# An encoder layer on one core: GpSimd splits and half a projection inside attention, and a reordered LN1 stage

## The chip, the cores and the metric

One core of a Trainium2 chip runs the whole kernel in one launch. The metric is device time in microseconds (us). A core has TensorE (PE: matmuls; PEld is its weight loads), VectorE (DVE), ScalarE (ACT), GpSimd (POOL) and SyncE (SP, which here only issues DMAs). Each works through its own instructions in order; semaphores tie them together. On chip, data lies in SBUF and matmul results in PSUM, which has eight banks of 128 x 512 f32.

## What is computed

The reference, cut to what matters (one layer, 1024 tokens of width 1024):

```
proj = x @ w_in                      # u | v | q
y_pool = pool_mixer(u)               # window means minus token, small matmul
y_conv = silu(LN(dwconv31(a * sigmoid(gate)) + b_dw))     # a, gate = split(v)
y_mem  = softmax(q k^T / sqrt(128)) v                     # 4 heads, 256 memory tokens
x = LN(alpha * x + concat(y_pool, y_conv, y_mem) @ w_out) # "LN1"
scores = sigmoid(x @ w_router); top-8 of 64 experts, gates normalised
x = LN(alpha * x + sum_experts gate * swiglu_e(x) + swiglu_shared(x))
```

## The kernel before

The 1024 tokens are 8 tiles of 128 (`NT = 8`). For accuracy every f32 operand of the large matmuls is kept as two parts, `hi` (rounded to the matmul's f32r format) and `lo` (the rest), and each product is three matmuls, hi·hi, hi·lo and lo·hi (`PRODS`). ScalarE makes the `hi` parts with a copy; the `lo` part is a subtraction, on VectorE nearly everywhere. So an operand passes ScalarE, then VectorE or GpSimd, before TensorE can read it.

All orders are written out by hand: each engine's block is a straight program, and what is said below is where its steps stand.

**Input projections.** `JOBS` lists 20 steps, the last six being q0, q1, pool0, pool1, q2, q3. For each weight block ScalarE's `split_hi` (L664) and VectorE's `split_lo` (L960) make `whl`. VectorE computes the depthwise convolution's 31 taps for two channel blocks between them (L1046, each 128 x 1024 from `glu` and `cv`), and the pooling sums. When the taps are done VectorE raises `s_cvd`.

**Attention.** For each tile t: ScalarE `q_hi` (L726) and `q_lo` (VectorE, L1120) split the query; TensorE `scores` (L1555, 12 matmuls of 128 x 256); VectorE `row_max` (L1126, L1129); ScalarE `exps` (L734); VectorE `probabilities` (L1143, two 128 x 512 products of two SBUF tensors); TensorE transposes them (L1579) into banks 4 and 5; ScalarE and VectorE make `pT` hi (L761) and lo (L1165). After tiles 3 and 7 the four heads' outputs are computed (L1591, 24 matmuls of 128 x 512 into banks 6 and 7 by turns), and ScalarE's `attention_out` (L743) takes them out. Between these steps lie the convolution's LayerNorm: `conv_mean` (PE L1528), `centre` (DVE L1093), `centred_squares` (ACT), `conv_variance` (PE L1536), `spread_rstd` (DVE L1103), `conv_rows` (PE L1544), `scale` (DVE L1109), and `conv_out` (ACT L712), which finishes `mixA`. In steps 4 to 7 the output weights `wo` are split in four quarters, `wo_hi` (ACT L717) and `wo_lo` (DVE L1115, 128 x 2048). GpSimd waits for `conv_out`, then makes constants and writes the empty lists with 11 DMAs (L540).

**LN1 stage.** For each tile: `mix_hi` (ACT) and `mix_lo` (POOL L552) split the mixed operand `mst`, in two halves (`mixA` and `qT`); `project` (PE L1604) is 24 matmuls of 128 x 512 for each of two column halves; VectorE adds the residual and takes statistics (L1252, L1255, L1259, L1261), GpSimd's `rstd` (L545) gives the inverse deviation, VectorE finishes x1 (L1264, L1267). TensorE transposes x1 (L1470, `x1_transposed`), ACT and DVE split it into `x1T` (L790, L1175, `x1_lo`), then TensorE runs the shared expert's gate and up (L1640, 24 matmuls of 128 x 512) and the router's `logits` (L1629, 24 of 128 x 64). VectorE's `route` (L1204 to L1225) picks experts, TensorE's `ranks` counts, VectorE's `rank` (L1182 to L1197) makes list addresses, and GpSimd's `scatter` writes them with 8 indirect DMAs for a tile (L559). PE's order in a step t is project(t+1, 0), ranks(t-1), project(t+1, 1), x1_transposed(t), shared_gate_up(t-1), logits(t).

**Experts.** When all lists are written, GpSimd reads them and gathers rows (L634, L605), and TensorE goes through the 64 experts' items (L1697, L1715).

## Time and profile before

| | |
|---|---|
| median of 3 runs | 1415.71 us (1411.47 to 1418.12) |
| the profiled execution, whole | 1413.44 us |
| its span, first to last instruction | 1411.8 us |
| TensorE busy | 1321.9 us, 94% of the span |
| VectorE, ScalarE, GpSimd busy | 68%, 57%, 33% |
| mean granted TensorE clock | 0.963 of 2.4 GHz |

The span is what the trace covers; 1.6 us of the execution lie around it. Times below are microseconds from the span's start. A row of the timeline gives start, duration, engine, line and operation, what is written and read, and, in brackets, how long the engine was idle just before and what released it. A row of merged instructions has their count behind an x. Rows of a window's table give busy time and count for each engine, then the mean granted clock, the DMA engines' share and GB/s.

### The profile page before, as it was taken

The numbers are of one execution on the slowest core, as the hardware profiler recorded it, in microseconds if no ns is written. First come the engines' busy times: TensorE is split into PE (matmuls) and PEld (weight loads), VectorE is DVE, ScalarE is ACT, GpSimd is POOL, SyncE is SP. The second block draws the span as 40 slices with busy tenths as digits, with TensorE's granted clock in tenths as the row PEclk, the third lists the DMA queues.
The fourth block names the chain that finished last, engine by engine and source line by source line (L and its number), as shares of the span: only waits on it lengthen the run. The fifth ranks groups of instructions, "written<-read, shape, count | busy, mean of one in ns | idle before, by whom it ended". The sixth has DMA issues, their size and how long they took to land.

```text
span 1411.8 us, 25745 instructions
## 1 busy us (share of the span) xinstructions
PE 1321.9 (94%) x6395; PEld 1092.1 (77%) x6396; DVE 960.6 (68%) x1121; ACT 797.7 (57%) x1056; POOL 471.7 (33%) x432
## 2 busy tenths in 40 slices
PE   8989776899997999999999999999999999999974
PEld 6877565688885888888888888888888888788851
DVE  5898886567673695865778457546759579677727
ACT  4122266212233686775777557547769678677724
POOL 0000002346654333433344333333334343433421
PEclk9999876899998999999999999999999999999988
DMA  6121202323357898988899889788889899999665
GB/s 242 45 75 60 119 1 97 105 76 90 87 168 219 313 355 292 359 254 284 276 328 358 254 252 287 236 260 264 287 291 345 259 331 335 341 328 301 196 179 233
DMA packets 77970, 324.13 MB, mean 230 GB/s; under 512 B 22560, under 2 KB 24768, under 8 KB 52720
## 3 DMA queue, kind: packets, MB, share of 16 engines
q1 hardware_dynamic: 43056, 251.05, 47.9%
q0 software_dynamic: 33728, 68.47, 20.7%
q10 hardware_dynamic: 1152, 4.19, 0.9%
q8 instruction: 17, 0.28, 0.1%
q14 instruction: 17, 0.14, 0.0%
HBM read 290.51 MB, written 67.72 MB: 254 GB/s over the span
## 4 chain that ended last, share of the span: by engine, by line
PE 64%; DMA 2%; issue 1%; DVE 1%; ACT 1%; ACTq 0%; SPq 0%; POOL 0%; POOLq 0%; DVEq 0%
PE ps L1697 38%; PE ps L1715 18%; PE ps L1470 6%; PE ps L1728 1%; DMA sum_d<-ysb,idx 1%; DMA late__121<-sum_d 1%; DVE acc L1427 0%; DMA xg<-x_d,idx 0%; DVE acc L1430 0%; DMA idx<-list_d 0%; DVE acc L1446 0%; ACT sq L930 0%; SPq L491 0%; ACT wgu L773 0%; POOL rs L654 0%
## 5 line engine op out<-in xcount | busy, mean ns | idle before, releaser
L1697 PE MATMUL ps<-wgu,xTe 128*128 x2304 | 551.9, 395 | 2.8 <-ACT wgu L773 1.2
L1697 PEld LDWEIGHTS ps<-wgu,xTe 128*128 128x128 f32 x2304 | 427.9, 189 | 90.9 <-issue 5.0
L615 POOL DMA_INDIRECT sum_d<-ysb,idx x95 | 176.6, 1859 | 512.1 <-ACT ysb L845 440.9
L1715 PE MATMUL ps<-wdn,hT 128*128 (+1 forms) x1236 | 299.7, 392 | 2.6 <-ACT hT L808 2.6
L1338 DVE TENSOR_TENSOR wgu<-raw,wgu (+1 forms) x128 | 287.6, 2288 | 8.5 <-issue 3.4
L1715 PEld LDWEIGHTS ps<-wdn,hT 128*128 128x128 f32 x1236 | 232.7, 189 | 51.3 <-ACT hT L808 3.0
L773 ACT CAST wgu<-raw (+1 forms) x128 | 246.8, 1929 | 7.1 <-SPq L430 4.9
L1343 DVE TENSOR_TENSOR xTe<-ps,xTe 128x512 fp32r<-128x512 f32 x194 | 124.4, 683 | 136.8 <-ACT xTe L840 136.8
L1338 DVE TENSOR_TENSOR wdn<-raw,wdn x64 | 146.7, 2292 | 59.1 <-ACT wdn L833 59.1
L845 ACT ACTIVATE ysb<-ps,idx 128x512 f32<-128x512 f32 x188 | 119.2, 686 | 118.6 <-PE ps L1715 118.6
L605 POOL DMA_INDIRECT xg<-x_d,idx x99 | 112.6, 1137 | 47.4 <-issue 32.8
L833 ACT CAST wdn<-raw x64 | 124.8, 1951 | 0.0
L891 ACT ACTIVATE hs<-ps 128x256 f32<-128x256 f32 x96 | 36.9, 384 | 146.2 <-PE ps L1697 146.2
L840 ACT CAST xTe<-ps 128x512 fp32r<-128x512 f32 x194 | 104.3, 598 | 11.4 <-PE ps L1470 11.0
L1495 PE MATMUL ps<-xT,whl 128*128 128x512 f32 x480 | 110.1, 390 | 0.0
L1470 PE MATMUL ps<-ident,xg 128*128 128x128 f32 x776 | 102.2, 275 | 5.4 <-DMA xg<-x_d,idx 3.4
L1470 PEld LDWEIGHTS ps<-ident,xg 128*128 128x128 f32 x776 | 91.6, 141 | 18.7 <-DMA xg<-x_d,idx 3.9
L1495 PEld LDWEIGHTS ps<-xT,whl 128*128 128x128 f32 x480 | 89.9, 188 | 19.2 <-issue 0.4
L1372 DVE TENSOR_TENSOR hx<-hs,ps 128x256 f32<-128x256 f32 x96 | 40.0, 417 | 93.1 <-ACT hs L891 93.0
L1604 PE MATMUL ps<-wo,mst 128*128 128x512 f32 x384 | 95.3, 409 | 4.0 <-POOL mst L552 4.0
L559 POOL DMA_INDIRECT list_d<-tg,addr x64 | 75.1, 1174 | 61.0 <-DVEq L1199 44.3
L1604 PEld LDWEIGHTS ps<-wo,mst 128*128 128x128 f32 x384 | 74.9, 198 | 20.2 <-issue 4.4
(230 smaller groups left out, 1149.8 us busy)
## 6 DMA issues: line engine op xcount, KB each, us to landing
raw<-in_w_gate SPq DMA_DIRECT2D x64, 1024.0 KB, 10.9
raw<-in_w_up SPq DMA_DIRECT2D x64, 1024.0 KB, 8.5
raw<-in_w_down SPq DMA_DIRECT2D x64, 1024.0 KB, 8.6
wraw<-in_w_in SPq DMA_DIRECT2D x10, 512.0 KB, 3.4
xin<-in_x SPq DMA_DIRECT2D x8, 512.0 KB, 7.4
wraw<-in_w_kv SPq DMA_DIRECT2D x8, 512.0 KB, 3.2
wor<-in_w_out SPq DMA_DIRECT2D x4, 1024.0 KB, 8.0
xres<-in_x SPq DMA_DIRECT2D x8, 512.0 KB, 5.2
```

Of the source, the lines that this page charges most:

```text
L605: g.indirect_dma_start(out=xg[:, c % 2], out_offset=None, in_=x1_d, in_offset=bass.IndirectOffsetOnAxis(ap=idx[:, c % RING, 0:1], axis=0), ...
L615: g.indirect_dma_start(out=sums, out_offset=bass.IndirectOffsetOnAxis(ap=idx[:, c % RING, c % 2:c % 2 + 1], axis=0), in_=ysb[:, c % 2], in ...
L773: nc.scalar.copy(wgu[:, v, 0, :, n * XD:(n + 1) * XD].rearrange("p a c n -> p (a c) n"), raw[:, bass.ds(slot_of(e, n), 1)].rearrange("p a ...
L833: nc.scalar.copy(wdn[:, v, 0].rearrange("p a c n -> p (a c) n"), raw[:, bass.ds(slot_of(e, 2), 1)].rearrange("p a (c n) -> p (a c) n", c=2 ...
L845: nc.scalar.activation(ysb[:, slot, b * 512:(b + 1) * 512], ps[:, bank + b, :], ACT.Copy, scale=scale).then_inc(s_y, 1)
L1338: V.tensor_tensor(dst, raw_, hi.bitcast(F), ALU.subtract).then_inc(done, 1)
L1343: last = V.tensor_tensor(xTe[:, s, 1, 4 * b:4 * b + 4], ps[:, b, :].rearrange("p (c n) -> p c n", c=4), xTe[:, s, 0, 4 * b:4 * b + 4].bitc ...
L1470: last = nc.tensor.transpose(ps[:, bank + c // 4, (c % 4) * 128:(c % 4 + 1) * 128], src[:, c * 128:(c + 1) * 128], ident[:])
L1495: last = mm(ps[:, b + h, :], wt[:, st, d], xT[:, mo, d, h * 512:(h + 1) * 512], start=(d == 0 and st == 0 and mo == 0), stop=(d == ND - 1 ...
L1604: last = mm(ps[:, 5 + h, :], mst[:, t % 2, st, c], wo[:, mo, c, h * 512:(h + 1) * 512], start=(c == 0 and st == 0 and mo == 0), stop=(c == ...
L1697: last = mm(ps[:, 2 + s, :], xTe[:, s, st, d], wgu[:, w, mo, d].rearrange("p a n -> p (a n)"), start=(d == 0 and st == 0 and mo == 0), sto ...
L1715: last = mm(ps[:, down_bank(i) + h, :], hT[:, s, st, c], wdn[:, w, mo, c, h * 512:(h + 1) * 512].rearrange("p a n -> p (a n)"), start=(c = ...
```

## The change

Two groups of edits.

*Attention.* The q and `wo` lo parts move from VectorE to GpSimd; `wo`'s quarters are loaded and split in the order 2, 3, 0, 1, starting in step 0. The fourth and last query weights' `split_hi(17)` stands before pool0's evacuation, no longer at q2. The mixed operands of tiles 0 and 1 get buffers of their own (`mst0`, `mst1`), and the half from `qT` (blocks 4 to 7) is split as soon as the first group's heads are out. TensorE runs blocks 4 to 7 of tile 0's projection in steps 4 and 5, into banks 6 and 7, and blocks 0 to 3 after the second group of heads. `scores(6)` and `scores(7)`, `conv_variance` and `conv_rows`, `variance`, `spread_rstd`, `scale` and `conv_out` stand at other steps. The second group's heads go to four banks (2, 3, 0, 1) and wait for no evacuation. GpSimd issues the list fills after its last `wo_lo`, and the constants after that. SP loads the first two residual tiles when the taps are done.

*LN1 stage.* TensorE's order in a step becomes project(t+1, 0), x1_transposed(t), ranks(t-1), project(t+1, 1), logits(t), shared_gate_up(t-1), with a written-out start. VectorE does `x1_lo(t-1)` right after the first half's statistics, `route` before `shared_hidden`, and the shared weights' lo (`shared_lo`) after the first `route`. ScalarE splits the shared weights after `x1_hi(0)`.

```
-                if w in W_JOBS and W_JOBS.index(w) < 17:
+                if w == "pool0":
+                    split_hi(17)
+                elif w in W_JOBS and W_JOBS.index(w) < 16:
                     split_hi(W_JOBS.index(w) + 1)
...
+            for t in range(4):
+                q_lo(t)
+            wo_lo(1, 2)
+            q_lo(4)
+            wo_lo(2, 3)
+            q_lo(5)
             g.wait_ge(s_norm_v, 1)
             g.tensor_tensor(rv[:, 1], rv[:, 0], half8[:], ALU.pow).then_inc(s_rstd, 1)
-
-            g.wait_ge(s_mix, 2)
+            q_lo(6)
+            q_lo(7)
+            wo_lo(3, 0)
+            mix_lo_half(1, 0, slice(4, 8))
+            mix_lo_half(2, 1, slice(4, 8))
+            wo_lo(4, 1)
+
+            for first in range(S, LIST, 8192):
...
+            g.wait_ge(s_norm_pe, 3)
...
-            mix_lo(0)
-            mix_lo(1)
-            g.wait_ge(s_fill, 16 * -(-(LIST - S) // 8192))
+            mix_lo_half(3, 0, slice(0, 4))
+            mix_lo_half(4, 1, slice(0, 4))
...
             for t in range(NT):
-                if t + 2 < NT:
-                    scores(t + 2)
-                if t == 1:
-                    conv_variance()
-                if t == 3:
-                    conv_rows()
-                    pe.wait_ge(s_yn, 1)
...
+                if t < 4:
+                    scores(t + 2)
+                if t == 4:
+                    scores(7)
+                probabilities_transposed(t)
+                if t == 1:
+                    conv_variance()
+                if t == 3:
+                    scores(6)
+                    pe.wait_ge(s_norm_v, 1)
+                    heads_out(0)
+                if t == 4:
+                    pe.wait_ge(s_wolo, 2)
+                    pe.wait_ge(s_olo, 1)
+                    pe.wait_ge(s_oe, HEADS)
+                    project_part(0, 0, range(4, 8), True, False)
+                if t == 5:
+                    project_part(0, 1, range(4, 8), True, False)
+                if t == 6:
+                    conv_rows()
+            heads_out(1)
+            pe.wait_ge(s_wolo, 4)
+            pe.wait_ge(s_olo, 3)
+            for h in range(2):
+                project_part(0, h, range(4), False, True).then_inc(s_pre_h if h == 0 else s_pre_pe, 1)
...
+            for t in range(2, NT - 1):
+                project(t + 1, 0)
                 x1_transposed(t)
...
+                ranks(t - 1)
+                project(t + 1, 1)
                 logits(t)
+                shared_gate_up(t - 1)
```

ScalarE at the end of the input projections, before: the split `whl<-wraw` of q3's weights is the row behind the two pool evacuations (`mixA`).

```order
L700 COPY qT<-ps 128x1024
L664 CAST whl<-wraw 128x1024
L700 COPY qT<-ps 128x1024
L703 ACTIVATE mixA<-ps,cpar 128x1024 x2
L664 CAST whl<-wraw 128x1024
L700 COPY qT<-ps 128x1024 x2
```

After:

```order
L744 COPY qT<-ps 128x1024
L706 CAST whl<-wraw 128x1024
L744 COPY qT<-ps 128x1024
L706 CAST whl<-wraw 128x1024
L747 ACTIVATE mixA<-ps,cpar 128x1024 x2
L744 COPY qT<-ps 128x1024 x2
```

The split now stands before both pool evacuations.

GpSimd from the end of its opening constants through attention, before:

```order
L523 TENSOR_TENSOR rv<-rv,half_143 128x8
L526 IOTA listE 128x64
L528 IOTA tokf 128x2
L530 IOTA itemp 128x2
L532 IOTA tg 128x64
L533 IOTA tg 128x64
L534 MEMSET ones_106 128x65
L535 MEMSET cumf 128x64
L536 MEMSET cumb 128x128
L540 DMA list_d<-fillw 128x192 x10
L540 DMA list_d<-fillw 128x96
L552 TENSOR_TENSOR mst<-mixA,mst 128x512
```

After, the same stretch up to the list fills; the iotas and memsets follow these, and then the `mixA` halves of tiles 0 and 1:

```order
L539 TENSOR_TENSOR qst<-qT,qst 128x512
L544 TENSOR_TENSOR wo<-wor,wo 128x2048
L539 TENSOR_TENSOR qst<-qT,qst 128x512
L561 TENSOR_TENSOR rv<-rv,half_145 128x8
L539 TENSOR_TENSOR qst<-qT,qst 128x512 x2
L544 TENSOR_TENSOR wo<-wor,wo 128x2048
L551 TENSOR_TENSOR mst_75<-qT,mst_75 128x512
L551 TENSOR_TENSOR mst_76<-qT,mst_76 128x512
L544 TENSOR_TENSOR wo<-wor,wo 128x2048
L571 DMA list_d<-fillw 128x192 x10
L571 DMA list_d<-fillw 128x96
```

GpSimd has twelve new splits, and the fills stand ahead of what TensorE's remaining half projection waits for.

VectorE in the LN1 stage after the change, from the start of tile 1 to the part of tile 2 that feeds the second logits (L1301 is the shared weights' lo, L1231 is `x1_lo`; of `route` only its last row, L1281, is shown, the ten ahead of it are left out):

```order
L1310 SCALAR_TENSOR_TENSOR xres<-xres,ps 128x512
L1313 BN_STATS stat<-xres 128x6
L1319 BN_AGGR mv<-stat 128x2
L1321 TENSOR_SCALAR mv<-mv 128x1
L1324 SCALAR_TENSOR_TENSOR xres<-xres,mv,g_86 128x1024
L1327 SCALAR_TENSOR_TENSOR xres<-xres,rs,b_87 128x1024
...
L1281 TENSOR_SCALAR msc<-msc,gs 128x64
L1301 TENSOR_TENSOR wsh<-wshr,wsh 128x8x256 x2
L1310 SCALAR_TENSOR_TENSOR xres<-xres,ps 128x512
L1313 BN_STATS stat<-xres 128x6
L1231 TENSOR_TENSOR x1T<-ps,x1T 128x512 x2
```

Before, the `wsh` rows stood ahead of tile 0's first row, and `x1T` behind each tile's L1261.

## Rows read from the trace of the kernel before

**Rows 1.** The page, part 1: busy us, share of the span, instructions.

```profile
PE 1321.9 (94%) x6395; PEld 1092.1 (77%) x6396; DVE 960.6 (68%) x1121; ACT 797.7 (57%) x1056; POOL 471.7 (33%) x432
```

**Rows 2.** Windows: busy us (instructions) by engine, PEclk, DMA share, GB/s.

```profile
165.00:174.00 9.00, 0.00 (x0) 0.00 (x0) 8.63 (x8) 2.59 (x4) 0.00 (x0) 0.70 0.96 381
183.00:211.00 28.00, 19.54 (x115) 16.81 (x113) 25.69 (x47) 17.49 (x46) 2.03 (x1) 0.79 0.00 1
211.00:251.00 40.00, 24.67 (x104) 19.48 (x104) 21.64 (x30) 27.83 (x53) 9.38 (x21) 0.71 0.28 98
251.00:276.00 25.00, 24.58 (x96) 20.09 (x97) 13.05 (x13) 4.86 (x4) 8.17 (x6) 0.87 0.31 106
276.00:297.00 21.00, 18.62 (x87) 15.52 (x86) 13.88 (x30) 3.60 (x6) 3.35 (x4) 0.84 0.20 76
460.00:1360.00 900.00, 895.98 (x4405) 750.16 (x4404) 614.55 (x575) 624.27 (x763) 342.69 (x286) 1.00 0.88 291
```

**Rows 3.** Timeline, end of the input projections, ScalarE's and VectorE's rows.

```profile
143.39 1.04 ACT L664 CAST whl<-wraw 128x1024 fp32r<-128x1024 f32 x1
144.46 1.22 DVE L960 TENSOR_TENSOR whl<-wraw,whl 128x1024 fp32r<-128x1024 f32 x1 [5.95 <-ACT whl L664]
158.88 14.49 DVE L1046 SCALAR_TENSOR_TENSOR cv<-glu,wdw,cv 128x1024 f32<-128x1024 f32 x11
```

**Rows 4.** Timeline, TensorE, attention and the first projection.

```profile
174.28 5.12 PE L1555 MATMUL ps<-kT,qst 128*128 128x256 f32 x24 [10.15 <-DVE qst L1120]
179.23 3.60 PE L1528 MATMUL ps<-cv,ones 128*128 128x512 f32 x8
...
186.69 1.26 PE L1579 MATMUL ps<-ident,pr 128*128 128x128 f32 x8 [2.44 <-DVE pr L1143]
...
206.40 1.97 PE L1579 MATMUL ps<-ident,pr 128*128 128x128 f32 x8 [2.94 <-DVEq L1111]
211.18 5.40 PE L1591 MATMUL ps<-pT,vv 128*128 128x512 f32 x12 [2.82 <-DVE pT L1165]
...
251.42 24.77 PE L1604 MATMUL ps<-wo,mst 128*128 128x512 f32 x96 [3.99 <-POOL mst L552]
```

**Rows 5.** Timeline, VectorE and GpSimd instructions that overlap, in the LN1 stage.

```profile
269.03 2.31 DVE L1267 SCALAR_TENSOR_TENSOR xres<-xres,rs,b 128x1024 f32<-128x1024 f32 x1 [0.47 <-POOL rs L545]
270.22 2.27 POOL L552 TENSOR_TENSOR mst<-qT,mst 128x512 fp32r<-128x512 f32 x1
...
308.37 2.89 DVE L1225 TENSOR_SCALAR msc<-msc,gs 128x64 f32<-128x64 f32 x1
308.67 1.29 POOL L552 TENSOR_TENSOR mst<-mixA,mst 128x512 fp32r<-128x512 f32 x1
```

**Rows 6.** Instructions writing `wo` and `mst`: ns min/median/max; then one timeline row.

```profile
L1115 DVE TENSOR_TENSOR wo<-wor,wo x4: 2278/2281/2291, 225.5 to 240.5; 128x2048 fp32r<-128x2048 f32 x4
L552 POOL TENSOR_TENSOR mst<-mixA,mst x8: 1263/1292/1721, 248.8 to 369.1; 128x512 fp32r<-128x512 f32 x8
...
214.10 6.14 POOL L540 DMA_DIRECT2D list_d<-fillw  x11 [0.32 <-POOL cumb L536]
```

**Rows 7.** Timeline, start of the LN1 stage, TensorE and VectorE.

```profile
259.57 4.49 DVE L1242 TENSOR_TENSOR wsh<-wshr,wsh 128x2048 fp32r<-128x2048 f32 x2 [7.74 <-ACT wsh L817]
279.45 3.76 PE L1629 MATMUL ps<-wrt,x1T 128*128 128x64 f32 x24 [2.38 <-DVE x1T L1175]
283.02 8.07 PE L1604 MATMUL ps<-wo,mst 128*128 128x512 f32 x24
...
305.50 5.71 PE L1604 MATMUL ps<-wo,mst 128*128 128x512 f32 x24
```

**Rows 8.** Timeline, the last addresses (VectorE) and GpSimd's last 16 scatters.

```profile
409.24 0.21 DVE L1182 TENSOR_TENSOR key<-listE,ps 128x64 f32<-128x64 f32 x1
413.21 0.97 POOL L559 DMA_INDIRECT list_d<-tg,addr  x1 [3.90 <-DVEq L1199]
...
435.57 0.97 POOL L559 DMA_INDIRECT list_d<-tg,addr  x1 [0.31 <-DMA list_d<-tg,addr]
```

281 lines of the change are left out of this document (165 added, 116 removed).

## The prediction

> **What bounds the kernel now.** I read the page's busy shares first: TensorE is busy for 94% of the span [rows 1]. Then the windows. From 460 to 1360 us TensorE is busy for 895.98 of 900 us at a granted clock of 1.00 [rows 2]. The change touches nothing there, so that stretch can only move as a block. What can be won is idle time and half-speed time ahead of it: TensorE is idle for all of 165 to 174, for 8.5 of 28 us from 183 to 211, for 15.3 of 40 from 211 to 251, and its clock there is 0.70 to 0.79, with short stretches at 0.87 and 0.84 behind [rows 2]. Last I read the timeline for what releases TensorE at each gap. In attention it is VectorE, which is busy for 25.69 of 28 us [rows 2]; at the first projection it is GpSimd's split of `mst` [rows 4]; in the LN1 stage, once, VectorE's split of `x1T` [rows 7]. The change moves VectorE's work away in the first place. So I follow one quantity: how many us of work TensorE is ahead of the old trace, at five points.
>
> **1. The taps.** VectorE sits idle 5.95 us for q3's `whl` hi part, which ScalarE makes at 143.39, behind both pool evacuations [rows 3]. Its source is there and q1 is done by 137, so in the new place it is made some 5.4 us earlier. The taps, which ran without a gap to 173.4 [rows 3], would end at 168.0. The first two q splits now run on GpSimd at 166 beside the taps. Whether that is free is the main question of this case. Rows 5 show two collisions. VectorE's L1267, two SBUF inputs, took 2.31 us where its neighbours take 1.28, while a GpSimd split ran; then that engine's next split took 2.27 instead of 1.29. And L1225, 64 columns wide and otherwise about 0.26 us, took 2.89 us, through two whole GpSimd splits (308.67 and its twin behind it). I read this as one engine waiting out the other's instruction. The taps have two SBUF inputs, so each of the two splits (1.29 us, [rows 6]) can hold them: end at 168.0 if none does, 170.6 if both do; I take 169.5.
>
> **2. To the first transposes (186.69 before, [rows 4]).** Scores 0 and 1 took 5.12 us and `conv_mean` 3.60 us at the low clock [rows 4]. Scores 0 can start at 168.1, so the mean ends near 176.8, `centre` (2.3 us) near 179.2, and the first probabilities (two of 0.65) near 180.5, or near 184.4 if the first `wo` split on GpSimd, which ScalarE's part releases at about 179, is in the way. I take 183.0: ahead by 3.7.
>
> **3. To the first heads (211.18 before, [rows 4]).** The old stretch is 24.5 us. VectorE loses four q splits, 0.6 each (-2.4). TensorE no longer waits in step 3 for `conv_rows` and `scale`: 2.94 us idle plus the rows' 1.98 (-4.9, [rows 4]). `scores(6)` is moved ahead of the heads (+1.7). New is what GpSimd's `wo` splits do to `probabilities`, which has two SBUF inputs. No row shows a 128 x 2048 split on GpSimd. VectorE's take 2281 ns [rows 6] against 0.68 for 128 x 512, a factor of 3.35, and four times as many columns bound it from above: 1.29 x 3.35 = 4.3 to 1.29 x 4 = 5.2; I take 4.6. Two of them start just as `probabilities` of steps 0 to 2 are due. Costs: 0 if they hold nothing, 9.2 if both hold in full; I take 6, since one may catch only the second half of a pair. Sum 24.5 - 2.4 - 4.9 + 1.7 + 6 = 24.9, so the heads start at 207.9: ahead by 3.3.
>
> The Trainium skill ("SBUF — State Buffer", Who interferes with whom) says that the port pair that VectorE and GpSimd share is an exclusive lock held for the whole instruction, and that a VectorE instruction with two SBUF inputs contends with one of GpSimd that reads SBUF. Rows 5 show that for splits of 1.29 us. By this rule the term of 6 would be up to 9.2 and the forecast 3 us later; without it the term is 0. The skill's measured price for such a GpSimd instruction of 2048 columns ("GPSIMD Engine Reference", Elementwise) is 4.5 us, by which the sum would hardly move.
>
> **4. To the rest of tile 0's projection.** From the heads on, one chain runs to ScalarE's split of tile 1's `qT` half: heads 8.7 (as 211.18 to 219.9 before, partly at half clock), scores(7) 1.7, transposes 1.1, two ScalarE copies and GpSimd's split 2.5, half of the half projection 3.7 (12 matmuls at 0.24, with some at half clock), transposes 1.0, the other 2.8, transposes 1.0, two copies 1.2: 23.7, so 231.6. From there GpSimd's own queue is longer than TensorE's: split 1.29, `wo` quarter 4.6, the 11 list fills 6.14 [rows 6], `conv_rows` long done, constants 1.0, `mixA` split 1.29: 14.3, so 245.9. TensorE itself has transposes 7 and the second heads done near 242 and waits some 4 us. So the `s_olo` wait of old (3.99 us, [rows 4]) is still there, now behind the fills. Before, project(0) began at 251.42 [rows 4]. Ahead by 5.5, and 24 of its 96 matmuls are done: 5.71 for 24 [rows 7]. Together 11.2.
>
> **5. The LN1 stage.** From the new start to the end of project(7, 1) TensorE has the same work, and the old trace loses 7.9 us there against full speed: the low clock at 251.42 (24.77 us for what takes 22.3, [rows 4]), the wait of 2.38, and 3.76 and 8.07 us for logits and projection that take 2.6 and 5.6 later [rows 7]. The new order removes the wait for `x1T` of tile 0, since project(2, 0) covers it. But what is late next is logits(1). On VectorE, between x1 of tile 1 and `x1_lo(1)`, stand `route(0)` (2.6 us, 4.6 where GpSimd's mst splits overlap it, as they did at 284), then `shared_lo`, 4.49 us [rows 7], then tile 2's first half, 1.5. Counted from the new start at 245.9, with 8.1 us for the first half projection at low clock, TensorE reaches logits(1) at 280.4; VectorE gets to x1 of tile 1 at 272.5, waits for logits(0) to 274, ends `route(0)` at 278.8, `shared_lo` at 283.3, and `x1_lo(1)` at 286.1. TensorE waits 5.7 us, and an idle of that kind was followed by matmuls at half speed before [rows 7], some 3.5 to 4.5 us more. With 2.5 for the cold start this is 12 to 13 against 7.9: I give back 5. From step 3 on VectorE's 16 us in a period of 20.15 leave it ahead; `rank` now stands ahead of `x1_lo`, 3.4 + 1.3 us against TensorE's 5.7 for the half projection beside them, which just fits.
>
> **6. The tail.** The chain from here is GpSimd's: 16 scatters at 1.28 us from 413.21 to 436.5, then the lists and the gathers [rows 8]. They start after `rank(6)` (409.24, [rows 8]), which was 16.0 us behind project(7, 1). Now logits(6) follows that projection at once and not behind the shared gate and up, `x1_lo(6)` is done earlier, and `rank(6)` comes 13.5 behind. That is a gain of 2.5, from 0 (if the last tile's addresses end it) to 3.
>
> **Sum.** 11.2 - 5 + 2.5 = 8.7 us. The profiled execution took 1413.44 (span 1411.8), which gives 1404.7. The median of the runs is 2.3 higher; I put the forecast at 1405.
>
> **Rivals.**
> *A, the splits on GpSimd hold nothing.* Against it are rows 5; for it, that many rows where the two engines overlap show no stretch. Then steps 1 to 3 bring 1.5 + 6 more, and the clock falls less often: 8 to 10 us more, 1396.
> *B, VectorE's order in the LN1 stage.* If `x1_lo` behind `rank` is late not once but in each of steps 2 to 6, by 0.5 to 1 us, TensorE loses 3 to 5 more and the clock may drop once again. For it: the fit is within 1 us. Against: VectorE has 4 us of slack a period. Time 1410.
> *C, slower.* GpSimd's `wo` splits take much more than 4.6 us because they and VectorE's instructions hold each other up in turn, as L1267 and its GpSimd partner did, both about a us longer [rows 5]. Three of the four stand on the path (two before the heads, the last before the remaining `mixA` split). At 7.5 us each the gain is gone; from 10 us each the kernel is over 0.5% slower, some 1421. Against it: one collision added 1 us to a GpSimd split, and each has at most four VectorE partners.
> *D, the moved work doesn't shorten attention at all,* because the chain through ScalarE (17.49 of 28 us busy [rows 2], with two `wo` hi parts of 1.9 added in it) takes VectorE's place: ahead only by the half projection, 5.6 - 5 + 2.5 = 3, so 1410 as in B.
>
> **How the numbers follow.** Forecast 0.50, A 0.26, B and D together 0.18, C 0.06. The forecast's own range is 1400 to 1409. A change within 0.5% (7 us) can't be told from none by such a measurement; that line lies at 1406.4 for the profiled execution, so about two thirds of the forecast's 0.50 are faster: 0.33, with A 0.59, and a little of B. Faster 0.61, same 0.33, slower 0.06. The range for 8 in 10 takes in most of A and of B: 1395 to 1411.
>
> **What would show it.** Step 1: L960 for q3 without idle ahead, taps ending at 168 to 171. Step 3: `probabilities` and GpSimd's 128 x 2048 rows, 4.3 to 5.2 us, with the product rows stretched to several us where they overlap; in rival A all of them stay at 0.69. Step 4: TensorE idle ahead of its last half projection, released by GpSimd, with the fills right ahead on GpSimd; rest starting near 246. Step 5: one gap of about 6 us at the second logits, behind `shared_lo`, and none later; in B one in each tile. Step 6: 16 scatters without a gap, starting 13 to 14 us behind project(7, 1). The 900 us of experts must keep their length; if that stretch changes by over 1 us, the whole account is wrong.

## The result

| | kernel before | changed kernel |
|---|---|---|
| median of 4 runs each | 1414.62 us (1411.47 to 1418.12) | 1397.47 us (1393.28 to 1397.76) |
| the profiled execution, whole | 1413.44 us | 1397.23 us |
| its span | 1411.8 us | 1395.6 us |
| mean granted TensorE clock | 0.963 | 0.972 |

The ratio is 0.9883, with a 95% interval of 0.9857 to 0.9909: 16 to 17 us faster, where 9 to 11 had been forecast. The direction and most of the mechanism were right; the gain in the profile was 16.2 us, nearly twice the 8.7 of the sum, and the time came near rival A's 1396, although A's mechanism did not hold.

The page, part 1, and three of the windows of [rows 2] for the changed kernel:

```profile
PE 1313.3 (94%) x6395; PEld 1088.9 (78%) x6396; DVE 951.9 (68%) x1109; ACT 792.9 (57%) x1053; POOL 500.1 (36%) x444
```

```profile
183.00:211.00 28.00, 23.58 (x131) 21.48 (x132) 27.19 (x38) 20.14 (x49) 18.05 (x8) 0.78 0.00 1
211.00:251.00 40.00, 30.06 (x131) 23.78 (x130) 16.17 (x27) 18.39 (x39) 16.98 (x25) 0.87 0.35 113
276.00:297.00 21.00, 15.64 (x61) 13.61 (x62) 14.27 (x32) 2.92 (x5) 8.49 (x8) 0.76 0.08 28
```

TensorE has the same matmuls (6395), but its busy time falls from 1321.9 to 1313.3 us: these 8.6 us of the gain are matmuls that ran at the higher clock. From 183 to 211 it works 23.58 us instead of 19.54, from 211 to 251 30.06 instead of 24.67 and at 0.87 instead of 0.71. In 276 to 297 it is worse than before (15.64 against 18.62 us, clock 0.76 against 0.84): that is the gap that the prediction placed there.

The same points in both traces, in us from the start of the span:

| | before | forecast | changed | ahead |
|---|---|---|---|---|
| taps end | 173.4 | 169.5 | 168.9 | 4.5 |
| first heads start | 211.2 | 207.9 | 205.8 | 5.4 |
| tile 0's last projection matmuls start | 251.4 | 245.9 | 241.1 | 10.3, and 24 matmuls done |
| tile 0's projection ends | 276.2 | | 260.4 | 15.8 |
| project(7, 1) ends | 397.4 | 391.2 | 386.7 | 10.8 |
| GpSimd's last scatter ends | 436.5 | 427.8 | 422.1 | 14.4 |
| first gate and up of an expert | 459.2 | | 445.9 | 13.3 |
| experts end | 1359.4 | | 1343.8 | 15.7 |
| span ends | 1411.8 | 1403.1 | 1395.6 | 16.2 |

The numbers of "changed" are starts and ends of rows in the next fences, or of rows of the same views. First the taps: one row of the timeline for ScalarE and one for GpSimd, the taps' durations (min/median/max), and TensorE's first row of attention.

```profile
138.04 1.05 ACT L706 CAST whl<-wraw 128x1024 fp32r<-128x1024 f32 x1
166.23 3.82 POOL L539 TENSOR_TENSOR qst<-qT,qst 128x512 fp32r<-128x512 f32 x2 [142.52 <-ACT qst L770]
```

```profile
L1120 DVE SCALAR_TENSOR_TENSOR cv<-glu,wdw,cv x60: 1276/1280/2167, 44.1 to 166.7; 128x1024 f32<-128x1024 f32 x60
```

```profile
167.88 4.63 PE L1620 MATMUL ps<-kT,qst 128*128 128x256 f32 x24 [3.51 <-POOL qst L539]
```

q3's hi part is there 5.35 us earlier, and one tap of 60, the last, takes 2167 ns instead of 1280, while GpSimd's two splits take 3.82 us instead of 2.6. TensorE's row is `scores(0)` and `scores(1)`: they no longer wait for the taps. They start 1.0 us before the taps end, released by GpSimd's q split, and 6.4 us earlier than before (174.28, behind VectorE's q split [rows 4]). Next, attention: VectorE's group `probabilities` from 174 to 252 us (busy, mean ns), then timeline rows where VectorE and GpSimd overlap.

```profile
L1204 DVE TENSOR_TENSOR pr<-pr,sm 128x512 f32<-128x512 f32 x16 | 19.0, 1230 | 0.3
```

```profile
178.69 5.61 DVE L1204 TENSOR_TENSOR pr<-pr,sm 128x512 f32<-128x512 f32 x2
178.74 5.02 POOL L544 TENSOR_TENSOR wo<-wor,wo 128x2048 fp32r<-128x2048 f32 x1 [1.62 <-ACT wo L761]
...
205.72 5.60 POOL L544 TENSOR_TENSOR wo<-wor,wo 128x2048 fp32r<-128x2048 f32 x1
208.07 3.28 DVE L1193 TENSOR_SCALAR sm<-sm 128x4 f32<-128x4 f32 x1
```

The same group in the kernel before:

```profile
L1143 DVE TENSOR_TENSOR pr<-pr,sm 128x512 f32<-128x512 f32 x16 | 10.3, 688 | 0.3
```

`probabilities` sums to 19.0 us where the same 16 instructions took 10.3 before, so GpSimd held it for 8.7 us, in two blocks of 4.3. The third `wo` split held a 128 x 4 `tensor_scalar` (L1193) for 3.1 us: 3.28 us for an instruction of 0.17. What is caught varies from execution to execution of the same orders: in the profiles of runs 7 and 11 the group takes 14.8 and 14.6 us, one of the two blocks is missing there, and yet the first heads start 35.5 and 36.7 us behind the taps, against 36.9 here. So a hold does not reach TensorE in full.

TensorE on its way through attention, and GpSimd's queue ahead of the rest of the projection:

```profile
179.44 0.66 PE L1633 MATMUL ps<-ident,pr 128*128 128x128 f32 x4 [1.81 <-DVE pr L1204]
184.36 1.11 PE L1633 MATMUL ps<-ident,pr 128*128 128x128 f32 x4 [4.26 <-DVE pr L1204]
...
205.81 5.76 PE L1647 MATMUL ps<-pT,vv 128*128 128x512 f32 x24 [1.08 <-DVE pT L1220]
216.51 4.37 PE L1656 MATMUL ps<-wo,mst 128*128 128x512 f32 x12 [2.63 <-issue]
...
241.07 19.29 PE L1656 MATMUL ps<-wo,mst 128*128 128x512 f32 x72 [4.30 <-POOL mst L551]
...
226.66 1.28 POOL L551 TENSOR_TENSOR mst<-qT,mst 128x512 fp32r<-128x512 f32 x1 [10.25 <-ACT mst L791]
227.89 4.55 POOL L544 TENSOR_TENSOR wo<-wor,wo 128x2048 fp32r<-128x2048 f32 x1
232.38 6.12 POOL L571 DMA_DIRECT2D list_d<-fillw  x11
239.66 2.49 POOL L551 TENSOR_TENSOR mst<-mixA,mst 128x512 fp32r<-128x512 f32 x2
```

Last, the LN1 stage and the tail (VectorE, TensorE, GpSimd, ScalarE). "Remote" as a releaser is an unknown queue: nothing that the trace names.

```profile
274.19 4.49 DVE L1301 TENSOR_TENSOR wsh<-wshr,wsh 128x2048 fp32r<-128x2048 f32 x2
280.04 1.27 DVE L1231 TENSOR_TENSOR x1T<-ps,x1T 128x512 fp32r<-128x512 f32 x2
281.36 5.33 PE L1725 MATMUL ps<-wrt,x1T 128*128 128x64 f32 x24 [5.58 <-DVE x1T L1231]
286.51 7.91 PE L1736 MATMUL ps<-wsh,x1T 128*128 128x512 f32 x24
...
399.77 0.97 POOL L600 DMA_INDIRECT list_d<-tg,addr  x1 [2.42 <-DVEq L1255]
421.14 0.97 POOL L600 DMA_INDIRECT list_d<-tg,addr  x1 [0.30 <-issue]
423.99 1.09 ACT L919 ACTIVATE ysb<-ps 128x512 f32<-128x512 f32 x2 [10.28 <-remote]
424.12 0.65 DVE L1393 CAST tab<-ps 1x480 int32<-1x480 f32 x1 [7.12 <-remote]
426.46 0.66 PE L1746 MATMUL ps<-ident,hxs 128*128 128x128 f32 x2 [6.13 <-DVE hT L1290]
445.87 8.38 PE L1798 MATMUL ps<-wgu,xTe 128*128 x24 [0.96 <-issue]
```

### The profile page after: what moved, and what is told of

Read it like the earlier page. It is cut to its first block, busy times and chain, and to the rows that moved or that the text cites. A ratio compares the mean times of both kernels' runs of the same rounds, so it can differ in the third digit from the quotient of the medians.

```text
span 1395.6 us, 25746 instructions
## 1 busy us (share of the span) xinstructions
PE 1313.3 (94%) x6395; PEld 1088.9 (78%) x6396; DVE 951.9 (68%) x1109; ACT 792.9 (57%) x1053; POOL 500.1 (36%) x444
## 4 chain that ended last, share of the span: by engine, by line
PE 82%; DVE 6%; DMA 4%; issue 2%; ACT 2%; POOL 1%; another core or an unknown queue 1%; ACTq 0%; SPq 0%; DVEq 0%; POOLq 0%
PE ps L1798 36%; PE ps L1816 18%; PE ps L1535 6%; PE ps L1656 6%; PE ps L1560 5%; PE ps L1736 3%; DMA raw<-in_w_up 3%; DVE cv L1120 2%; PE ps L1725 2%; PE ps L1829 1%; DVE pr L1204 1%; PE ps L1572 1%; DMA xin<-in_x 1%; DMA sum_d<-ysb,idx 1%
## 5 line engine op out<-in xcount | busy, mean ns | idle before, releaser
L965 ACT ACTIVATE hs<-ps 128x256 f32<-128x256 f32 x96 | 36.9, 384 | 147.1 <-PE ps L1798 147.0
L1535 PEld LDWEIGHTS ps<-ident,xg 128*128 128x128 f32 x776 | 90.3, 140 | 14.8 <-DVE xTe L1408 2.2
```

What stands on the lines that cost most here:

```text
L1535: last = nc.tensor.transpose(ps[:, bank + c // 4, (c % 4) * 128:(c % 4 + 1) * 128], src[:, c * 128:(c + 1) * 128], ident[:])
```

## The experiments

All ratios are to the kernel before, measured on the same chip. The changed kernel was not measured again beside them, so differences to it are given by the medians and by the two ratios, where they differ. The start of the program differs a little from execution to execution: the taps end between 167.0 and 169.0 us in the profiles of the kernels that have the early split. Distances between two points of one profile are therefore used below where a few us matter. They scatter too: the first heads start 35.5 to 36.9 us behind the taps in nine profiles in which attention's orders up to there are those of the changed kernel.

### 1. The early split alone

The kernel before, with q3's hi part ahead of pool0's evacuation and nothing else.

```
-                if w in W_JOBS and W_JOBS.index(w) < 17:
+                if w == "pool0":
+                    split_hi(17)
+                elif w in W_JOBS and W_JOBS.index(w) < 16:
```

> The kernel before with one edit: q3's hi part (ScalarE) stands ahead of pool0's evacuation. Theory (VectorE's idle 5.95 us is removed and the taps are on the path): taps end at 168.0 instead of 173.4, first transposes at 186.69 - 4 to 5, and since nothing is on GpSimd in attention there, most of it reaches the end: 4 to 5 us faster, some 1410. Rival (TensorE's chain of scores and conv_mean, or ScalarE, takes VectorE's place at once): first transposes under 1.5 us earlier, time the same within 1.5 us.

Measured: 1408.44 us (1403.83 to 1410.75, ten runs) against 1412.78, ratio 0.9965 (0.9948 to 0.9982). The taps end at 168.0, the projection starts at 247.4 instead of 251.4, project(7, 1) ends 5.7 us earlier. So step 1 is worth 4 to 5 us of the 16 to 17 by itself (2.5 to 7.3 by the interval). What is left, 11 to 12, comes from the rest.

### 2. The LN1 order alone

The kernel before with the second group of edits (TensorE's, VectorE's and ScalarE's order in the LN1 stage).

```
             for t in range(2, NT - 1):
                 project(t + 1, 0)
                 x1_transposed(t)
...
+                ranks(t - 1)
+                project(t + 1, 1)
                 logits(t)
+                shared_gate_up(t - 1)
```

> The kernel before with the LN1 stage's new order alone (TensorE, VectorE, ScalarE); attention untouched. Theory (the new order makes logits(1) wait for shared_lo, 5.6 us and a low clock behind it, and starts the 16 last scatters 3 us earlier behind project(7, 1)): the stage from project(0) to the end of project(7, 1) is 149 to 152 us instead of 145.8, the scatters start 13 instead of 16 us behind it, so 1 to 3 us slower than before. Rival (the order itself brings a good part of the 17 us): 4 to 8 us faster.

Measured: 1414.66 us, ratio 1.0017 (0.9999 to 1.0036). The forecast had this group at 5 us given back and 2.5 won in the tail. In this profile TensorE waits at the second logits as in the changed kernel:

```profile
290.35 4.49 DVE L1252 TENSOR_TENSOR wsh<-wshr,wsh 128x2048 fp32r<-128x2048 f32 x2
297.52 5.33 PE L1647 MATMUL ps<-wrt,x1T 128*128 128x64 f32 x24 [5.57 <-DVE x1T L1182]
...
396.76 5.73 PE L1620 MATMUL ps<-wo,mst 128*128 128x512 f32 x24
```

The last row is project(7, 1). It ends at 402.5 instead of 397.4, the scatters start 13.1 us behind it instead of 15.8, and GpSimd's last scatter ends at 438.0 instead of 436.5. The new order gains nothing by itself: it costs 5.1 us up to the end of project(7, 1), as the prediction had it, and wins 3.6 of them back by the last scatter. As far as the two groups add, all of the gain of the whole change comes from ahead of the LN1 stage.

### 3. The list fills behind the splits

The changed kernel, with GpSimd's 11 list fills behind its `mixA` splits of tiles 0 and 1.

```
-            for first in range(S, LIST, 8192):
-                ...
             g.wait_ge(s_norm_pe, 3)
...
             mix_lo_half(3, 0, slice(0, 4))
             mix_lo_half(4, 1, slice(0, 4))
+            for first in range(S, LIST, 8192):
+                ...
```

> The changed kernel with GpSimd's 11 list fills behind the two mixA splits of tiles 0 and 1, the only edit. Theory (the 4.30 us that TensorE waits at the rest of tile 0's projection is GpSimd's queue, the fills are 6.1 us of it): the wait is gone or under 0.5 us, the projection starts at 236.8 instead of 241.07, at full clock or nearly, 4 to 6 us faster than the changed kernel, ratio to before 0.985. Rival (what is late next, the loads of g1, b1 or the weights of the shared expert, or the statistics of tile 0 behind the fills, takes it back): under 1.5 us.

Measured: 1391.23 us (1391.09 to 1391.61), ratio 0.9853 (0.983 to 0.9877): under the changed kernel by 6.2 us in the medians, and by 4.2 if the two ratios are compared. GpSimd's and TensorE's rows:

```profile
232.77 6.14 POOL L604 DMA_DIRECT2D list_d<-fillw  x11
234.76 16.48 PE L1655 MATMUL ps<-wo,mst 128*128 128x512 f32 x72
```

The wait of 4.30 us ahead of the rest of the projection is gone, and so is the cold start: 16.48 us for the 72 matmuls instead of 19.29. From the end of the taps to the start of these matmuls it is 67.7 us instead of 72.2. The prediction's reading of this place (GpSimd's queue, with the fills in it, is what TensorE waits for) is shown.

### 4. x1_lo(1) first

```
-                    if b == 0 and t >= 1:
+                    if b == 0 and t >= 1 and t != 2:
                         x1_lo(t - 1)
...
                 if t == 1:
+                    x1_lo(1)
                     shared_lo()
```

> The changed kernel with x1_lo(1) on VectorE ahead of shared_lo, the only edit. Theory (logits(1) waits 5.58 us for shared_lo's 4.49 us and tile 2's first half): logits(1) starts without a wait, the shared gate and up of tile 0 then waits under 2.5 us for shared_lo, and the clock keeps its high level; project(7, 1) ends 6 to 9 us earlier and the kernel is as much faster. Rival (the wait only moves to the shared gate and up, since shared_lo is as long there): under 2 us.

Measured: 1397.02 us (1395.58 to 1400.77), ratio 0.9903 (0.9875 to 0.9931): nothing gained, where 6 to 9 us had been expected. The wait at the second logits is gone, but others stand in its place (GpSimd, then TensorE at the third logits):

```profile
283.08 1.68 POOL L600 DMA_INDIRECT list_d<-tg,addr  x1 [14.07 <-DVEq L1255]
288.64 0.59 POOL L589 TENSOR_TENSOR rs<-mv,neghalf 128x1 f32<-128x1 f32 x1
...
301.96 5.33 PE L1726 MATMUL ps<-wrt,x1T 128*128 128x64 f32 x24 [4.38 <-DVE x1T L1231]
```

VectorE comes to tile 0's addresses only behind `shared_lo`. GpSimd starts its scatters at 283.08, and the rstd of tile 2 (L589, ready at 282.6) has to stand behind four of them until 288.64. TensorE waits 1.46 us for `shared_lo` at the first shared gate and up, 1.7 for x1 of tile 2, and 4.38 for its split. The stretch from the start of the 72 matmuls to the end of project(7, 1) is 147.9 us, against 145.6 in the changed kernel.

### 5. GpSimd's wo splits in four pieces

```
-                g.tensor_tensor(wo[:, 1, 2 * n:2 * n + 2], wor[:, 2 * n:2 * n + 2],
-                                wo[:, 0, 2 * n:2 * n + 2].bitcast(F), ALU.subtract)
+                for c in (2 * n, 2 * n + 1):
+                    for k in (0, 512):
+                        last = g.tensor_tensor(wo[:, 1, c, k:k + 512], wor[:, c, k:k + 512],
+                                               wo[:, 0, c, k:k + 512].bitcast(F), ALU.subtract)
```

> The changed kernel with each of GpSimd's four 128 x 2048 wo splits issued as four instructions of 128 x 512. Theory (a GpSimd instruction holds VectorE's two-input instruction until it ends, so the length of one instruction is the length of the hold): no `probabilities` row longer than about 2.6 us where the changed kernel has 5.0 to 5.6, the first heads start 2 to 5 us before 205.8, and the kernel is 1 to 4 us faster than the changed one, a ratio of 0.985 to 0.988 to the kernel before. Rival (the two engines share the port by bytes, whatever the instruction): VectorE's products are stretched by the same total, first heads at 205 to 206, no gain. Second rival (they alternate and each piece is stretched): GpSimd's splits sum to over 7 us each, and the kernel is 0 to 3 us slower than the changed one.

Measured: 1396.61 us (1394.74 to 1401.04), ratio 0.9892 (0.9861 to 0.9923): no gain. VectorE, GpSimd, TensorE:

```profile
177.59 2.38 DVE L1207 TENSOR_TENSOR pr<-pr,sm 128x512 f32<-128x512 f32 x2
177.94 5.63 POOL L546 TENSOR_TENSOR wo<-wor,wo 128x512 fp32r<-128x512 f32 x4 [1.62 <-ACT wo L764]
187.94 6.83 PE L1604 MATMUL ps<-ones,buf 128*128 128x1 f32 x32
```

The hold does shrink with the instruction: the pairs of `probabilities` take 2.38, 3.32 and 3.31 us ahead of the heads where the changed kernel has 5.61 and 5.64 (the longest single one 1.78 us, against 5.03 in the changed kernel). That part of the theory stands. But more pairs are caught (the 16 products are held for 7.2 us in all, against 8.7), and GpSimd's work grows from 5.02, 4.60 and 5.60 to 5.63, 5.40 and 6.48 us. TensorE reaches `conv_variance` 20.1 us behind the taps, where the changed kernel has 20.3, and does it wholly at the low clock (6.83 us, against 4.12). The first heads start 38.4 us behind the taps, against 36.9. The time on the path was not bought back. A run without that stretch of low clock might have gained; none shows it.

### 6. Without the half projection

The changed kernel; TensorE does all eight blocks of tile 0 behind the second heads.

```
-                if t == 4:
-                    ...
-                    project_part(0, 0, range(4, 8), True, False)
-                if t == 5:
-                    project_part(0, 1, range(4, 8), True, False)
...
-                project_part(0, h, range(4), False, True)
+                project_part(0, h, (4, 5, 6, 7, 0, 1, 2, 3), True, True)
```

> The changed kernel without the half projection between attention's steps: TensorE runs all eight blocks of tile 0's projection behind the second heads. Rival (the prediction's step 4: 24 matmuls, 5.7 us, are hidden beside GpSimd's queue): 4 to 6 us slower than the changed kernel. Theory (in attention TensorE's own chain leads to ScalarE's split of tile 1's qT half, and from there GpSimd's queue of 14.4 us sets the start; the 24 matmuls stand on that chain, so taking them out brings the start of the projection forward by about what it has to do more): start of tile 0's projection at 233 to 236 instead of 241.1, and a time within 2 us of the changed kernel's.

Measured: 1397.71 us (1394.63 to 1399.65), ratio 0.9883 (0.9857 to 0.9909), the changed kernel's own. TensorE's row of the projection:

```profile
236.86 23.38 PE L1656 MATMUL ps<-wo,mst 128*128 128x512 f32 x96 [3.53 <-POOL mst L551]
```

Its start, 236.86, is just outside the 233 to 236 that had been expected. It starts 67.8 us behind the taps instead of 72.2 and ends 91.2 us behind them instead of 91.4. The 24 matmuls moved into attention stand on the chain that leads to ScalarE's split of tile 1's qT half, and so to GpSimd's queue; taken out, that queue starts at 222.47, 16.5 us behind the first heads instead of 20.9, and TensorE has 4.1 us more to do later (23.38 against 19.29). The half projection, 5.7 us of the forecast, is worth nothing here, within the some 4 us by which either ratio is uncertain.

### 7. x1_lo(1) first, and rstd ahead of the scatters

As 4, and GpSimd does the rstd of tile 2 ahead of tile 0's scatters.

```
             for t in range(NT):
+                if t == 2:
+                    rstd(4)
+                    scatter(0)
-                if t >= 2:
+                elif t >= 2:
                     scatter(t - 2, range(K // 2))
-                rstd(t + 2)
+                if t != 2:
+                    rstd(t + 2)
```

> The changed kernel with VectorE's x1_lo(1) ahead of shared_lo, as in the run before, and with GpSimd's rstd of tile 2 ahead of tile 0's first four scatters. Theory (the earlier run gained nothing since x1 of tile 2 then waited 5.5 us for a rstd behind four scatters, and the third logits 4.4 us behind that): no wait over 2 us on TensorE from the start of tile 0's projection to the end of project(7, 1), that stretch 138 to 141 us instead of 145.6, and 3 to 6 us faster than the changed kernel. Rival (VectorE is short of time in this stretch whatever the order, since route, shared_lo, rank and x1_lo of tiles 0 to 2 all fall due within 20 us): another wait of 3 us or more in steps 2 or 3, and less than 2 us gained.

Measured: 1393.67 us (1385.46 to 1397.25), ratio 0.9851 (0.9806 to 0.9896). By the medians that is 3.8 us under the changed kernel, by the ratios 4.5, but the four runs spread over 12 us and the two intervals overlap, so the time alone does not show a gain. No wait over 2 us is left, but the stretch is 143.2 us, not 138 to 141:

```profile
277.45 7.33 PE L1741 MATMUL ps<-wsh,x1T 128*128 128x512 f32 x24 [1.46 <-DVE wsh L1305]
318.00 4.02 PE L1730 MATMUL ps<-wrt,x1T 128*128 128x64 f32 x24 [1.23 <-DVE x1T L1235]
```

Two waits of 1.46 and 1.23 us remain, each followed by matmuls at the low clock (7.33 us for 24 that take 5.7, 4.02 for 24 that take 2.76, and 7.82 behind them). What comes behind these waits costs more than the waits themselves: 1.6 us behind 1.46, 3.4 behind 1.23. Against 144.0, 144.1 and 145.6 in three profiles of kernels with the changed kernel's LN1 order and its cold start (runs 5 and 8, and the changed kernel) this is 0.8 to 2.4 us.

### 8. A pause in the tail

GpSimd waits for VectorE's item tables between the scatters of tile 6 and of tile 7.

```
             scatter(NT - 2)
+            g.wait_ge(s_tabs, 1)
             scatter(NT - 1)
```

> The changed kernel in which GpSimd waits for VectorE's item tables between the eight scatters of tile 6 and the eight of tile 7. In the changed kernel VectorE's copy of the tables (L1393) and ScalarE's evacuation of the second shared output (L919) stand idle 7.1 and 10.3 us for nothing the trace names, and go on 1.9 to 2 us after GpSimd's last scatter. Theory (what these two engines lack comes to them only when GpSimd's run of indirect DMAs has ended): with the pause both go on within 3 us of the last scatter of tile 6, so before 416 instead of 424, and the last scatter is out by 428; the time is within 4 us of the changed kernel's. Rival (the wait belongs to a point in time or to the weight loads, not to the scatters): VectorE still waits until about 424, the last eight scatters end at 434 or later, and the kernel is 6 to 10 us slower than the changed one.

Measured: 1395.87 us (two runs), ratio 0.9877 (0.9847 to 0.9908). VectorE, GpSimd, TensorE:

```profile
412.84 0.65 DVE L1394 CAST tab<-ps 1x480 int32<-1x480 f32 x1
414.53 0.97 POOL L600 DMA_INDIRECT list_d<-tg,addr  x1 [6.67 <-DVEq L1400]
438.71 1.97 PE L1536 MATMUL ps<-ident,xg 128*128 128x128 f32 x8 [10.07 <-DMA xg<-x_d,idx]
```

VectorE's copy of the tables runs at 412.84, 4.98 us behind the last scatter of tile 6 and with no unnamed wait; ScalarE has none either. In the changed kernel and in all ten other variants of this study without a pause, the last such wait ends 2.0 to 2.4 us behind GpSimd's last scatter (424.12 behind 422.11 in the changed kernel). So in these it goes with the end of the run of scatters and not with a time. It does not come with every such run: the kernel before has 16 scatters too and no unnamed wait, and copies its tables at 429.35, in the middle of them. And the pause doesn't pay here: the last scatter ends 45.2 us behind project(7, 1) instead of 35.5, more than the pause of 6.67, and TensorE idles 10.07 us for the gathered rows.

### 9. wo on VectorE

The changed kernel with the four `wo` lo parts back on VectorE, in steps 0, 1, 4 and 5.

```
+                if t in (0, 1, 4, 5):
+                    nth, n = {0: (1, 2), 1: (2, 3), 4: (3, 0), 5: (4, 1)}[t]
+                    v.wait_ge(s_wohi, nth)
+                    V.tensor_tensor(wo[:, 1, 2 * n:2 * n + 2], wor[:, 2 * n:2 * n + 2],
+                                    wo[:, 0, 2 * n:2 * n + 2].bitcast(F), ALU.subtract).then_inc(s_wolo, 1)
```

> The changed kernel with the four wo lo parts (128 x 2048) given back to VectorE, one in each of steps 0, 1, 4 and 5; the q splits stay on GpSimd. VectorE then has 4 x 2.28 us more work and is no longer held: in the changed kernel three of GpSimd's four splits hold it for 4.3, 4.3 and 3.1 us. Theory (held time and given work are worth about the same, so moving wo to GpSimd brought nothing on the path ahead of the first heads): first heads start within 2 us of the changed kernel's 205.8; behind them GpSimd's queue to the rest of the projection is 4.55 us shorter, so that projection starts 2 to 5 us earlier than 241.1, and the kernel is 1 to 4 us faster than the changed one. Rival (GpSimd's splits are worth having, since VectorE's step is what bounds attention): first heads 3 us or more later than 205.8, and a time equal to the changed kernel's or up to 4 us slower.

Measured: 1391.79 us (1390.4 to 1394.31), ratio 0.9846 (0.9827 to 0.9865): 5.7 us under the changed kernel by the medians, 5.2 by the ratios, more than the theory's 1 to 4. VectorE, GpSimd, TensorE:

```profile
185.21 2.27 DVE L1222 TENSOR_TENSOR wo<-wor,wo 128x2048 fp32r<-128x2048 f32 x1
226.85 6.12 POOL L565 DMA_DIRECT2D list_d<-fillw  x11
237.67 16.49 PE L1655 MATMUL ps<-wo,mst 128*128 128x512 f32 x72
```

The first heads start 35.5 us behind the taps (36.9 in the changed kernel): VectorE does two of its four splits, at 2.27 us each, ahead of them and is still not later. That it is ahead is not shown, since run 7, with the changed kernel's attention, has 35.5 as well. Behind the heads GpSimd's queue is shorter by 4.55 us and done when TensorE arrives: the wait of 4.30 us is gone, and the 72 matmuls take 16.49 us instead of 19.29. This is the same wait that run 3 removes in another way, and the two were not tried together. So moving `wo` to GpSimd cost time in this queue, with the fills in it; the rest of the attention group more than made up for it.

### 10. Late fills without the half projection

Edits 3 and 6 together.

> The changed kernel with the 11 list fills behind GpSimd's last splits of tiles 0 and 1 (as in the third run) and also without the half projection in attention (as in the sixth). With GpSimd's queue shortened by 6.1 us it is no longer what sets the start of the projection; TensorE's own chain does. Theory: now the half projection is hidden work that pays, and leaving it out costs what it takes, so this kernel is 3 to 6 us slower than the one with late fills alone (ratio near 0.989 against 0.9853). Rival (it is worth nothing here either, as in the sixth run): within 1.5 us of the late fills alone.

Measured: 1391.38 us (1388.29 to 1396.82), ratio 0.9859 (0.9834 to 0.9884), against 1391.23 with late fills alone. TensorE:

```profile
231.99 21.93 PE L1655 MATMUL ps<-wo,mst 128*128 128x512 f32 x96
```

The theory falls, the rival holds. The projection ends 85.9 us behind the taps; with the half projection (run 3) it is 84.2. That is 1.7 us of profile and none in the medians. The 24 matmuls take 5.45 us out of the later block (21.93 against 16.48), but with them the second heads start 2.3 us later, and take 7.15 us against 5.74 here, part of them at the low clock.

### 11. Late fills, x1_lo(1) and rstd first

Edits 3 and 7 together, five runs.

> The changed kernel with three moves: the 11 fills behind the splits, x1_lo(1) ahead of shared_lo, rstd of tile 2 ahead of tile 0's scatters. Theory: the gains of the third run (6 us) and of the seventh (0 to 4 us, 2.4 in the profiled stretch) add, since one ends before the projection starts and the other begins behind it: 6 to 9 us faster than the changed kernel, ratio 0.981 to 0.985. Rival (the third run's earlier start brings VectorE's work on tile 0 and 1 closer together, and the LN1 stage gives the gain back): no faster than the late fills alone, 0.985 or more.

Measured: 1388.08 us (1386.48 to 1393.18), ratio 0.9821 (0.9804 to 0.9837): 9.4 us under the changed kernel by the medians, 8.8 by the ratios. Against run 3 it is 3.2 us by the medians and 4.5 by the ratios. The LN1 stretch is 141.0 us against 142.8 in run 3. The gains add, as far as the spread lets one say so.

### 12. With a short pause

As 11, and GpSimd waits between the two last tiles' scatters for ScalarE's third `hidden_hi`, which comes earlier than the tables.

```
             scatter(NT - 2)
+            g.wait_ge(s_hhi, 3)
             scatter(NT - 1)
```

> The kernel of the eleventh run (late fills, x1_lo(1) and rstd first) with a pause in GpSimd's tail that is shorter than the eighth run's: between the scatters of tile 6 and those of tile 7 it waits for ScalarE's third hidden_hi, some 1.5 to 2 us, where it waited 6.67 us for the tables before. Theory (a gap of that size in the run of indirect DMAs is enough for ScalarE and VectorE to get what they lack): no idle over 2 us with no named cause on ScalarE and VectorE in the tail, idx read within 4 us of the last scatter instead of 7, first gate and up 57 to 58 us behind the end of project(7, 1) instead of 59 to 62, and 0 to 3 us faster than the eleventh run, a ratio of 0.980 to 0.982. Rival (they need the whole pause of 6.67 us): the unnamed waits are back and end some 2 us behind the last scatter, which is 1.5 to 2 us later than in the eleventh run; a time equal to it or up to 2 us slower, 0.982 to 0.984.

Measured: 1387.43 us (1385.56 to 1392.84), ratio 0.9829 (0.9807 to 0.985). GpSimd, ScalarE, GpSimd, TensorE:

```profile
402.83 0.97 POOL L595 DMA_INDIRECT list_d<-tg,addr  x1 [3.10 <-ACT hT L881]
410.80 1.08 ACT L923 ACTIVATE ysb<-ps 128x512 f32<-128x512 f32 x2 [0.95 <-remote]
420.29 1.74 POOL L680 DMA_DIRECT2D idx<-list_d  x3 [6.53 <-issue]
433.61 6.71 PE L1803 MATMUL ps<-wgu,xTe 128*128 x24
```

With a pause of 3.10 us the longest unnamed wait in this profile is 0.95 us. The first gate and up stands 58.5 us behind the end of project(7, 1), against 61.2 in run 11 and 59.2 in the changed kernel. The lists are read 6.5 us behind the last scatter, not within 4 as expected, and the first gate and up is just outside the 57 to 58 us. By the times, 1387.4 against 1388.1 and a ratio of 0.9829 against 0.9821, nothing can be told from run 11. These two are the fastest kernels of the study, 8 to 10 us under the changed one and 24 to 26 under the kernel before.

## Why the prediction was right, and where it was short

**Step 1** held: 168.9 instead of 169.5, one tap held where up to two had been allowed for.

**Steps 2 and 3.** The holding of `probabilities` was 8.7 us, against 2.5 and 6 in the sums: right in kind and in size. It was divided otherwise, 4.3 in each stretch, so the transposes were complete later than forecast and the stretch from 184.36 to the heads took 21.5 us instead of 24.9. Rival A (the splits hold nothing) is out; that the time came near its 1396 is chance. The first part of the transposes is at 179.44 already, since only the second product of the pair is caught; the second part waits until 184.36. The heads are 2.1 us earlier than forecast. Two things the prediction didn't ask. Run 9: is the held time less than the work that was moved? It is not (8.7 and 3.1 us held for 9.1 moved). Runs 7 and 11: does a hold arrive at the heads in full, as the sum had it? In run 11 one of 4.3 us less moved them by 0.2.

**Step 4** is where the sum was short. The forecast had tile 0's projection 11.2 us ahead; it was 15.8 at its end. GpSimd's queue started at 226.66 instead of 231.6. Of these 4.9 us, 2.1 come from before the heads. The other 2.8 are a term that was mis-sized: the chain from the heads to this queue was put at 23.7 us and took 20.9 (205.81 to 226.66), because the heads went through in 5.76 us instead of 8.7. The 8.7 had been taken from the old trace, where the first 12 matmuls ran at the low clock (5.40 us [rows 4], granted clock 0.51 from 211.2 to 216.5) and only the other 12 at the full one (1.00 from 217 to 220):

```profile
216.96 3.02 PE L1591 MATMUL ps<-pT,vv 128*128 128x512 f32 x12 [0.38 <-ACT qT L743]
```

In the changed kernel the clock was 1.00 for all 24, from 205.8 to 211.5. The queue itself was right to 0.1 us: 14.4 (226.66 to 241.07) against 14.3, and TensorE waited 4.30 us against "some 4".

A reason was wrong as well, though the sum did not suffer from it. It credits 5.71 us for 24 matmuls done early, and rival D counts them as a gain that stays. The rows show them done; runs 6 and 10 show that this is worth 0 to 2 us, because the same matmuls delay the queue that sets the start. The forecast's own chain has them in it, at 3.7 and 2.8 us, so it had charged what it credited. It had the right place for the wait and the wrong reason for half of its gain.

**Step 5** held: given back 5.1 us (project(7, 1) ends 121.2 us behind tile 0's projection before, 126.3 after) against 5, and the wait at logits(1) was 5.58 us against 5.7, behind `route(0)` and `shared_lo` as written. No later gap: rival B is out. The terms fit less closely than their difference. The old loss, put at 7.9 us, adds up to 8.5 from the terms named for it, and the new one, put at 12 to 13, was 13.2: 2.8 at the cold start, the wait of 5.58, and 2.6 and 2.2 behind it. Run 2 shows the same cost, 5.1 us, when the group stands alone.

**Step 6** held in its place: the scatters start 13.1 us behind project(7, 1) against 15.8 before, a gain of 2.7 (forecast 2.5). The prediction gives its 16.0 and 13.5 for `rank(6)`, but they are distances of the scatters: the row of `rank(6)` at 409.24 is 11.8 us behind. And 16 scatters are not 16 times 1.28 us; they took 23.3 us before and 22.3 now, which is another 1.0. What step 6 missed lies behind: the last scatter is 14.4 us ahead, the first gate and up 13.3. ScalarE and VectorE stand still for 10.3 and 7.1 us in the tail, TensorE then waits 6.13 us for `hT` at 426.46, and its shared down projections last until 440.5, where the kernel before stood idle for 3.45 us for the gathered rows.

**The experts** did not keep their length, as demanded: from the first gate and up to their end 897.9 us against 900.2. In the other profiles of this study it is 895.2 to 900.3, so this stretch moves by 5 us between kernels that do the same there, and the old 900.2 was at the long end. By the prediction's own test the account is off by more than 1 us there. The start does not explain it: the first gate and up was slower in the changed kernel (8.38 us against 7.09), not faster. What makes the difference stays open.

**Sum**, ahead: 15.8 (forecast 11.2), less 5.1 (5), plus 3.6 by the last scatter (2.5), less 1.1 in the handover to the experts (0), plus 2.4 in the experts (0), plus 0.5 behind them: 16.2. The forecast was 8.7. Step 4 carries 4.6 of the 7.5 missed; the experts' length, which the prediction did not claim, 2.4. The sum is for the profiled execution (1404.7 against 1397.23); the forecast of 1405 took it over without the 2.3 us by which it says the median lies higher.

Rival C (GpSimd's `wo` splits take 7.5 to 10 us) is out: 4.55 to 5.60. The Trainium skill ("GPSIMD Engine Reference", Elementwise) states 4.5 us for such an instruction; the undisturbed one here took 4.55. Rival D is out as a whole: attention did get shorter, and not by the half projection, which D had counted as its one gain.

What stays open: the attention group has more edits than were taken apart. The early split is worth 4 to 5 us, the half projection 0 to 2, GpSimd's `wo` splits minus 5 in a queue that also has the fills. What is left, some 15 us of the group's gain (15.8, less 4.5, plus 5.2 to 5.7, less 0 to 2, if these add), belongs to the q splits on GpSimd, the new places of the convolution's steps, the early split of the `qT` halves and the four banks of the second heads; none of these was tried alone. The rows say where it lies. The first heads start 36.9 us behind the taps, against 37.8 before and 38.8 in run 1, so hardly any of it is won ahead of them. From the first heads to the end of tile 0's projection it is 54.5 us against 65.0, and 54.3 without the half projection (run 6).

## What to carry to other kernels

Work that is moved onto an idle engine is free only if that engine isn't in someone's queue later and doesn't lock anyone out: here the moved `wo` splits took 8.7 and 3.1 us of holding and 4.55 us of queue to save 9.1 us of VectorE, and giving them back won 5 to 6 us. Before matmuls are credited as "done early", ask what the chain through them releases; if the wait behind them is set by another engine whose start they delay, they are worth nothing. And a wait removed by reordering can come back a step later: here 5.58 us at the second logits became 1.46, 1.7 and 4.38 us, until the third engine in the ring (GpSimd's rstd behind its scatters) was moved as well.
